# A bias table stored as one row per head, projection tiles among the gating unit's steps, dilated keys multiplied during the first attention, and pooled rows stored ahead of the table's loads

## The reference

```python
def mixer(x):                     # x (1024, 1024) for the prompt, (8, 1024) for the samples
    qa, ka, va, fa, ub, vb, qc, kc, vc, pd = split(x @ w_in)      # 2052 columns
    logf = log_sigmoid(fa + b_forget)
    o_a = forgetting_attention(qa, ka, va, cumsum(logf))          # 4 heads x 64, causal
    v = layer_norm(gelu(vb), g, b)                                # per token, 256 channels
    o_b = gelu(ub) * (tril(w_spatial) @ v + b_spatial)            # per 128-token chunk, 4 groups
    o_c = dilated_attention(qc, kc, vc, t5_table)                 # offsets (128,1),(512,4),(2048,16)
    o_d = pooled(pd) @ w_pool                                     # trailing means 2/4/8/16 minus pd
    return (sigmoid(x @ w_gate) * branches(o_a, o_b, o_c, o_d)).sum(-2) @ w_out
x = layer_norm(ALPHA * x + mixer(x)); x = layer_norm(ALPHA * x + moe(x))   # 16 experts, top 2
```

## Time and profile before

| | |
|---|---|
| median of 3 runs | 1512.75 us (1506.55 to 1513.86) |
| the profiled execution | 1514.06 us |
| its span, first to last instruction | 1512.1 us |
| PE busy | 1371.3 us (91%) |
| PE waits over 2 us named below | 10.4, 9.4 and 2.7 us |
| chain that ended last | PE 83%, DMA 5%, DVE 4%, ACT 3% |

### The profile page before, as it was taken

One profiled execution on the slowest core, in us unless ns is written; L12 is line 12 of the kernel. 1 busy time (PEld: TensorE's weight loads), 2 busy tenths in 40 slices (PEclk: granted clock), 3 DMA queues, 4 the chain that ended last, 5 costly groups with the idle time before them and its releaser, 6 DMA issues.

```text
span 1512.1 us, 20414 instructions
## 1 busy us (share of the span) xinstructions
PE 1371.3 (91%) x7682; PEld 1094.0 (72%) x7682; DVE 779.9 (52%) x1336; ACT 480.7 (32%) x788; POOL 322.8 (21%) x233
## 2 busy tenths in 40 slices
PE   6989989979788999999999999999928999999970
PEld 5665565756555799999999999778826666677640
DVE  3465474542245422344444344464775677777746
ACT  3311145421136311111111111221125556555636
POOL 0258910353453000000000000000245112223220
PEclk9989999999979999999999999999959999999995
DMA  7347620355601121321321431422387998887645
GB/s 226 117 134 263 212 98 1 107 182 169 221 17 32 64 81 63 108 80 64 107 80 65 144 126 66 150 78 79 122 311 280 379 310 312 297 310 254 202 153 226
DMA packets 75197, 237.72 MB, mean 157 GB/s; under 512 B 17029, under 2 KB 27476, under 8 KB 61422
## 3 DMA queue, kind: packets, MB, share of 16 engines
q1 hardware_dynamic: 48630, 160.73, 29.7%
q0 software_dynamic: 17792, 59.20, 13.2%
q10 hardware_dynamic: 8704, 16.84, 3.2%
HBM read 213.49 MB, written 65.74 MB: 185 GB/s over the span
## 4 chain that ended last, share of the span: by engine, by line
PE 83%; DMA 5%; DVE 4%; ACT 3%; issue 2%; POOL 2%; SPq 0%; DVEq 0%; POOLq 0%
PE ps L481 16%; PE ps L483 16%; PE ps L482 16%; PE ps L620 7%; PE ps L1257 6%; PE ps L1229 5%; PE ps L1253 2%; PE ps L1354 2%; PE ps L1254 2%; PE ps L1397 2%; PE ps L1255 2%; DMA b<-in_state_k 2%; PE ps L545 1%; DMA out_pool_p<-b 1%; DMA tmp_yd<-b,b 1%
## 5 line engine op out<-in xcount | busy, mean ns | idle before, releaser
L481 PE MATMUL ps<-b,b 128*128 128x344 f32 (+1 forms) x1360 | 469.1, 345 | 5.4 <-DVE b L841 2.7
L483 PE MATMUL ps<-b,b 128*128 128x344 f32 (+1 forms) x1360 | 465.1, 342 | 0.0
L482 PE MATMUL ps<-b,b 128*128 128x344 f32 (+1 forms) x1360 | 464.9, 342 | 0.0
L481 PEld LDWEIGHTS ps<-b,b 128*128 128x128 f32 x1360 | 254.9, 187 | 24.5 <-issue 3.5
L483 PEld LDWEIGHTS ps<-b,b 128*128 128x128 f32 x1360 | 254.6, 187 | 19.2 <-issue 0.9
L482 PEld LDWEIGHTS ps<-b,b 128*128 128x128 f32 x1360 | 254.6, 187 | 17.2 <-issue 0.9
L1012 DVE TENSOR_TENSOR b<-b,b 128x2048 fp32r<-128x2048 f32 x64 | 146.6, 2291 | 66.2 <-ACT b L704 60.0
L649 ACT ACTIVATE b<-ps,b 128x344 f32<-128x344 f32 x96 | 52.7, 549 | 380.2 <-PE ps L483 380.2
L1083 POOL DMA_INDIRECT tmp_xs<-b,b x36 | 43.1, 1198 | 593.1 <-issue 572.4
L1229 PE MATMUL ps<-b,b 128*128 128x128 f32 (+1 forms) x782 | 119.1, 285 | 39.2 <-DMA b<-tmp_xs 18.4
L1229 PEld LDWEIGHTS ps<-b,b 128*128 128x128 f32 (+1 forms) x782 | 93.0, 145 | 83.4 <-issue 35.6
(11 more groups left out here) (290 smaller groups left out, 1556.0 us busy)
## 6 DMA issues: line engine op xcount, KB each, us to landing
b<-in_w SPq DMA_DIRECT2D x96, 1024.0 KB
b<-in_w_merge SPq DMA_DIRECT2D x32, 640.5 KB, 4.3
tmp_xs<-b ACTq DMA_DIRECT2D x32, 514.0 KB, 4.3
b<-tmp_xs SPq DMA_DIRECT2D x32, 514.0 KB
b<-in_w_in SPq DMA_DIRECT2D x8, 1024.0 KB, 8.8
b<-in_xT SPq DMA_DIRECT2D x4, 1024.0 KB, 11.9
b<-in_w_out SPq DMA_DIRECT2D x4, 1024.0 KB, 8.2
b<-in_x SPq DMA_DIRECT2D x8, 512.0 KB, 4.0
```

The costliest lines, as they stand in the source:

```text
L481: mm(out, hi, mhi, start=start, stop=False)
L482: mm(out, hi, mlo, start=False, stop=False)
L483: return mm(out, lo, mhi, start=False, stop=stop)
```

## The change

- The bias table is computed once per head on 4 partitions (3 matmuls of all 4 heads' columns, 512, 512 and 128 wide), copied by ACT in 3 pieces to `tb_row`, and stored by one transfer that reads each of the 4 rows 128 times. POOL and DVE no longer wait for that store before their next steps; POOL waits for `tb_src` instead.
- "vfa" tiles 2 to 7 and then 0 and 1 are projected between the table, the spatial matmuls and the transposes of `o_b`. The norm of `v` takes two fused instructions per tile in place of three, the first of them already in the loop over tiles.
- The dilated keys of the samples are loaded, multiplied and summed during the first attention (rounds 6 to 13), in a buffer that the key products have left. POOL's later loop holds value gathers alone. ACT's split of the weights of "vpd" starts while the last "qkc" tile is projected.
- The 15 pooling rows are stored before the four loads of the table, and these wait for the last eviction rather than the last projection.
- At the end of the merge the sample tile's split moves to DVE, and all but its last eighth is done before the last merge step.

```diff
-PROJECTED = ([("uv", t) for t in TILE_ORDER] + [("vfa", NT), ("qka", NT)] + [("vfa", t) for t in TILE_ORDER[1:]]
+VFA_ORDER = (2, 3, 4, 5, 6, 7, 0, 1)
+PROJECTED = ([("uv", t) for t in TILE_ORDER] + [("vfa", NT)] + [("vfa", t) for t in VFA_ORDER[:2]] + [("qka", NT)]
+             + [("vfa", t) for t in VFA_ORDER[2:]]
...
-        kc = at(RING + TOKB, [P, 2, 3, W])
+        kc = at(OT + 3 * (TOKB // 4), [P, 2, 3, W])
-        tb_src = at(OT + 4608, [P, 4, TBW])
+        tb_row = at(PSB, [H, TBW])
+        KEYS_C = (6, 7, 8, 9, 10, 11, 12, 13)
...  (end of the merge, PE and DVE)
-                pe.wait_ge(S("mlo"), s + 1)
+                pe.wait_ge(S("mlo"), s + 2 if s else 1)
...
-            for u in range(2):
-                merge_weight(KD // 2 - 1, 3, u, u == 1)
-                split_out_weights(KD - 2 + u, KD - 1 + u)
+            merge_weight(KD // 2 - 1, 3, 0, False)
+            split_out_weights(KD - 2, KD - 1)
+            split_out_weights(KD - 1, KD)
+            first_tile(slice(0, KD - 1))
+            merge_weight(KD // 2 - 1, 3, 1, True)
...  (SP)
-            sp.wait_ge(S("tb_src"), 12)
-            sp.dma_start(a["tb_dram"].rearrange("h (p u) -> p h u", p=P), tb_src[:]).then_inc(S("tb_out"), 16)
+            sp.wait_ge(S("tb_src"), 1)
+            sp.dma_start(a["tb_dram"].rearrange("h (p u) -> h p u", p=P),
+                         tb_row[:].rearrange("h (o u) -> h o u", o=1).to_broadcast([H, P, TBW])).then_inc(S("tb_out"), 16)
...
-            sp.wait_ge(S("proj"), 45)
+            sp.wait_ge(S("evicted"), pj_index("vpd", NT - 1) + 1)
+            sp.dma_start(a["pool_p"], vp[P - 15:P, NT - 1, W:2 * W]).then_inc(S("out_pool"), 16)
             for h in range(H):
                 src = a["tb_dram"][h, P - 1:P - 1 + P * (TBW - 1)].rearrange("(p u) -> p u", u=TBW - 1)[:, 0:SEQ]
                 sp.dma_start(tb[:, h, :], src).then_inc(S("tb_in"), 16)
-            sp.wait_ge(S("evicted"), pj_index("vpd", NT - 1) + 1)
             sp.dma_start(a["v_c_p"].rearrange("(t p) w -> p t w", p=P), vp[:, :, 0:W]).then_inc(S("out_vc"), 16)
-            sp.dma_start(a["pool_p"], vp[P - 15:P, NT - 1, W:2 * W]).then_inc(S("out_pool"), 16)
...  (PE)
-            for h in range(H):
-                for q in range(3):
-                    n = h * 3 + q
-                    if n >= 2:
-                        pe.wait_ge(S("tb_src"), n - 1)
-                    mm(ps[:, 6 + n % 2, 0:384], t5[:, h:h + 1].to_broadcast([NBUCK + 1, P]), oh_rev[:, q * 384:(q + 1) * 384],
-                       start=True, stop=True).then_inc(S("tb_mm"), 1)
+            for n, (lo, hi) in enumerate(TB_PARTS):
+                m = mm(ps[0:H, 5 + n, 0:hi - lo], t5[:], oh_rev[:, lo:hi], start=True, stop=True)
+            m.then_inc(S("tb_mm"), 1)
...
+            project("vfa", NT)
+            project("vfa", VFA_ORDER[0])
+            project("vfa", VFA_ORDER[1])
+            project("qka", NT)
+            spatial(0)
+            spatial(1)
+            project("vfa", VFA_ORDER[2])
+            spatial(2)
+            spatial(3)
+            project("vfa", VFA_ORDER[3])
+            ob_transposes(0, 1)
+            project("vfa", VFA_ORDER[4])
+            ob_transposes(2, 3)
...
+            ob_transposes(6, 7, 8)
+            project("vfa", VFA_ORDER[7])
...  (ACT)
-                    if i == 1:
+                    if t == VFA_ORDER[6]:
                         act.wait_ge(S("obT"), NT + 1)
                         act.wait_ge(S("out_vb"), 16)
...
                 if chunk == "qkc":
-                    act.wait_ge(S("ks"), 16)
-                if chunk == "vpd":
-                    act.wait_ge(S("proj"), pj_index("qkc", NT - 1) + 1)
+                    act.wait_ge(S("ks"), 24)
                 for k in range(KD):
+                    if chunk == "vpd" and k < KD - 1:
+                        act.wait_ge(S("pk"), k + 1)
...  (DVE)
+                v = uv[0:r, t, W:2 * W]
+                dve.scalar_tensor_tensor(v, v, mv[0:r, t, 0:1], gbB[0:r, 0, :], ALU.subtract, ALU.mult)
...
-            for t in range(NT + 1):
+            for t in range(NT, -1, -1):
                 r = rows(t)
                 v = uv[0:r, t, W:2 * W]
-                link(dve.tensor_scalar(v, v, mv[0:r, t, 0:1], rs[0:r, t:t + 1], ALU.subtract, ALU.mult))
-                link(dve.tensor_tensor(v, v, gbB[0:r, 0, :], ALU.mult))
-                link(dve.tensor_tensor(v, v, gbB[0:r, 1, :], ALU.add))
+                m = dve.scalar_tensor_tensor(v, v, rs[0:r, t:t + 1], gbB[0:r, 1, :], ALU.mult, ALU.add)
...
-            dve.wait_ge(S("tb_out"), 16)
             to_oT(1, "ob_tr", "obT")
...
-            last_a = attention(0, lambda h, qt: fb[:, h, 0:P * (qt + 1)], side_a)
+            def side_keys(u):
+                side_a(u)
+                if u in KEYS_C:
+                    key_sums_c(KEYS_C.index(u))
+            last_a = attention(0, lambda h, qt: fb[:, h, 0:P * (qt + 1)], side_keys)
...  (POOL)
-            pool.wait_ge(S("tb_out"), 16)
+            pool.wait_ge(S("tb_src"), 2)
...
-            pool.wait_ge(S("pv"), 8)
+            pool.wait_ge(S("ks"), 16)
             keys_c(0)
             keys_c(1)
             pool.wait_ge(S("sd_qkc"), 16)
             load_q(NB, 0, SC["qkc"])
-            key_step_c(0)
-            key_step_c(1)
+            for b in range(NB):
+                if 0 < b < NB - 1:
+                    pool.wait_ge(S("ks"), 16 + b)
+                    keys_c(b + 1)
+                key_step_c(b)
             for s in range(2, 16):
                 pool.wait_ge(S("dv"), s - 1)
                 load_values(s)
-                if s < NB:
-                    pool.wait_ge(S("ks"), 16 + s - 1)
-                    keys_c(s)
-                    key_step_c(s)
```

More of the change, by code:

```diff
@@ L517, in y_half @@
                 for k in range(KD):
+                    if s == 0 and n == 0 and k == KD - 1:
+                        pe.wait_ge(S("mlo"), 2)
                     if n == 1 and s == 0:
@@ L1255, in project @@
                         m = mm(ps[:, j % 2, :], lo, whi, start=False, stop=(k == KD - 1))
+                        if chunk == "qkc" and t == NT - 1 and k < KD - 1:
+                            m.then_inc(S("pk"), 1)
                     else:
@@ L1275, in _, with spatial @@
+            m.then_inc(S("tb_mm"), 1)
             for i in range(4):
-                m = mm(ps[:, 6, i * H:(i + 1) * H], oh_dec[:, i, :], t5[:], start=True, stop=True)
+                m = mm(ps[:, 4, i * H:(i + 1) * H], oh_dec[:, i, :], t5[:], start=True, stop=True)
             m.then_inc(S("tb_mm"), 1)
-            project("vfa", NT)
-            project("qka", NT)
-            pe.wait_ge(S("wsp_m"), 4)
-            pe.wait_ge(S("v_done"), 1)
-            for g in range(4):
-                if g >= 2:
-                    pe.wait_ge(S("ob"), g - 1)
-                elif g == 0:
-                    pe.wait_ge(S("tb_src"), 13)
+            def spatial(g):
+                if g == 0:
+                    pe.wait_ge(S("wsp_m"), 4)
+                    pe.wait_ge(S("v_done"), 1)
+                    pe.wait_ge(S("tb_src"), 1)
+                elif g >= 2:
+                    pe.wait_ge(S("ob"), g)
@@ L1288, in _, with ob_transposes @@
                 mm(ps[:, 6 + g % 2, :].rearrange("p (t c) -> p t c", t=NT), wsp[:, g, :],
                    uv[:, 0:NT, W + 64 * g:W + 64 * g + 64], start=True, stop=True).then_inc(S("band_mm"), 1)
-            pe.wait_ge(S("ob"), 5)
-            for t in range(NT + 1):
-                if t >= 2:
-                    pe.wait_ge(S("obT"), t - 1)
-                r = rows(t)
-                for f in range(2):
-                    m = tr(ps[:, 4 + t % 2, f * P:f * P + r], uv[0:r, t, f * P:(f + 1) * P], r)
-                m.then_inc(S("ob_tr"), 1)
+            def ob_transposes(*tiles):
+                for t in tiles:
+                    if t == 0:
+                        pe.wait_ge(S("ob"), 5)
+                        pe.wait_ge(S("tb_src"), 2)
+                    if t >= 2:
+                        pe.wait_ge(S("obT"), t - 1)
+                    r = rows(t)
+                    for f in range(2):
+                        m = tr(ps[:, 4 + t % 2, f * P:f * P + r], uv[0:r, t, f * P:(f + 1) * P], r)
+                    m.then_inc(S("ob_tr"), 1)
@@ new lines, in _ @@
+            project("vfa", NT)
[11 more added lines that the diff above has]
+            ob_transposes(2, 3)
+            project("vfa", VFA_ORDER[5])
+            ob_transposes(4, 5)
@@ L1299, in qk_transposes @@
+            project("vfa", VFA_ORDER[6])
+            ob_transposes(6, 7, 8)
+            project("vfa", VFA_ORDER[7])
             def qk_transposes(chunk, t, base):
@@ L1312, in qk_transposes @@
                 m.then_inc(S(f"qk_tr_{chunk}"), 1)
-            for t in TILE_ORDER[1:]:
-                project("vfa", t)
             for i, t in enumerate(TILE_ORDER):
@@ L1630, in _ @@
             act.activation(rs[:], rs2[:], ACT.Sqrt).then_inc(S("sd"), 1)
```

(22 more changed lines are left out.)

42 lines of the change are left out of this document (23 added, 19 removed).

## The result

| | before | changed |
|---|---|---|
| median | 1513.3 us (4 runs) | 1556.28 us (4 runs, 1555.53 to 1557.55) |
| ratio | | 1.0289, 95% interval 1.0259 to 1.0319 |
| span of the profiled execution | 1512.1 us | 1554.9 us |

A forecast was written before the change was run, and what follows sets the result against it. PE (busy 91%) was taken as the engine to shorten, with POOL's key products limiting from 90 to 200 us. Terms -2 -11 +3 -14 -2 = -26 took 1514.06 to 1488, forecast 1487 on the median, range 1478 to 1497.

The forecast's parts named there:

- the landing of the store: Bias-table store: one engine per source row, four at 25.5 GB/s each, data taking 23 us, landing at about 97.
- rival 2: Bias-table store: four neighbouring rows together get 25.5 GB/s, landing at about 166; 1554 or 1553 us; chance 0.20.
- Price of that landing: Late table store: POOL's first product at 170 instead of 89.97, first attention begins 64 us late.
- First attention's start without the slow store: Table and gating unit: of 14 us gained on PE, 2.8 arrive; taken as -2 (bounds -4 and +1).
- Dilated keys: Leaving POOL's later loop: PE's value-step waits go, -11 (bounds -12, -8); first attention pays +3 (bounds 0, +8).
- Pooled rows: Stored before the table's loads: PE's 10.4 us idle plus 3.6 of clock, -14 (bounds -10, -18).
- End of the merge: Of 2.7 us lost there, one short pair of DVE instructions stays: -2 (bounds -2.7, 0).
- The sum: Whole kernel: terms total -26, 1514.06 becomes 1488, forecast 1487 on the median, range 1478 to 1497.

The follow-up runs named there:

- 128 rows: Changed kernel with the table's rows computed on 128 partitions, each stored 4 times, instead of 4 partitions 128 times: 1482.44 us, ratio 0.9801.
- the probe: Kernel before with seven 2304 KB stores added behind its end, read from 4 to 128 partitions: 92.2 us from 4 neighbouring, 5.9 from 128.
- the value tiles together: Kernel on 128 rows with the value tiles projected together behind the gating unit, as before the change: 1473.23 us, ratio 0.9748.

## Why the prediction was wrong

- **The step that failed** is the landing of the store: "So I take one engine per row, four in all", each at 25.5 GB/s, landing at about 97. The count of engines was right (24% of 16). Their rate was not: four neighbouring source rows have 25.5 GB/s together, and the store landed at 164. That is rival 2, which stood at 0.20 and gave 1553; 1556.28 was measured. That these are so near is in part luck: 70.5 us were lost where it had 64, and 27.7 won behind that where it had 24. The row that spoke against it, the 8 packets of the earlier trace rows, was a load into SBUF of one packet per partition with no stream behind it. By their recorded times these 8 packets moved 76 GB/s to eight neighbouring partitions, more than the 51 of the store from eight; why a load should do better was not tested, and it was no row to size a store by. The rule that spoke for the rival (the Trainium skill, "SBUF — State Buffer", Door 1) has 27.6 GB/s, measured, for partitions 0 to 3; the trace now has 25.5. Against it I had no row of a store with few source rows, and a fifth was too small a chance.
- **Price of that landing.** Named: POOL's first product at 170 and 64 us late; measured 169.04 and 70.5. POOL's part was right: its fifteenth product ended at 261.9. What had no price was PE's own path, and it came out longer: 61.4 us behind `out_vb` in the same queue, two tiles of "qka", 25.2 behind the forget gates, then six more tiles up to the first score, with about 3 us of waiting in all. The two waits also cost clock: a tile of "qka" takes 7.03 us where the granted clock is 1.00 (100 to 197 in the kernel before), and took 8.86 behind the second wait, at 0.76 (206.7 to 216.5).
- **First attention's start without the slow store.** Forecast: third product 111.3, first score 196.3, 16th sum ended 201.6, a gain of 2.8. Measured on 128 rows: 109.08, 196.93, 202.55, a gain of 2.2. Right in number, and in part in its reason: the 14 us of PE time do meet a chain of POOL and DVE. But they meet it at the fifth key sum, not at the end of the 16 products. PE stops there for 15.6 us and then runs to its first score with about 3 us of waiting in all. I did not see that stop, nor that the interleaving itself costs 9.2.
- **Dilated keys.** -11 for PE's waits, measured -12.6 with the early split of the weights; +3 in the first attention, measured +2.7 to +3.1. Right.
- **Pooled rows.** -14, measured -13.5 alone and -14.3 in the stage with the rest. The wait as foretold, the clock only in part: foretold was near 1.0 for 25 us where the earlier trace rows has 0.73, and measured were 0.93 with this edit alone, 0.86 on 128 rows (399 to 424) and 0.80 in the changed kernel (473 to 498).
- **End of the merge.** -2, measured -3.3 by the profiles, 0.6 past its bound of -2.7.
- **The sum** without the slow store, 1487, was measured at 1482.44, inside its own range of 1478 to 1497 (28.9 below the kernel before on the same chip, where 26 was forecast). The upper end of that range does not follow from the bounds: +1, -8, +8, -10 and 0 add up to -9, which is 1504 and not 1497. The 1482.44 are inside either way.

## What to carry to other kernels

A store is sized by its bytes and by the SBUF partitions it reads: in all seven stores of the probe no four neighbouring partitions gave more than some 25.5 GB/s together, however often their rows were repeated, and spreading the rows (here for no instruction more than one small copy) gives the rate back. A slow transfer must be priced by what stands behind it in its queue and by what else uses its engines. And engine time saved ahead of a chain that another engine sets is to be followed until it arrives; where it does not, look at the written order of the engine between them.

## What the runs showed of the hardware beyond that

- A transfer from four neighbouring partitions slows other queues too: in the kernel with the store on ACT's queue, 16 KB took 18 us to land, and a gather of keys 21.3 instead of 5.9.
- Some of DVE's small operations take far longer while POOL multiplies. The copy within SBUF below does, and so does the forget gates' first step above (3.64 us at 200.30, beside POOL's product at 199.37). Key sums do not: in the changed kernel one took 2.29 us beside a product (173.58) and one 2.28 without (272.91). Nor did a copy out of PSUM, 0.41 us for 128x256 at 216.81, beside a product. Why was not tested. With the value tiles together, a copy of 128x480 took 4.96 us beside a product of POOL, and 0.41 without one in the kernel on 128 rows; these rows are of the two kernels in that order:

```profile
89.30 4.96 DVE L1873 COPY b<-b 128x480 f32<-128x480 f32 x1
```

```profile
103.14 0.41 DVE L1887 COPY b<-b 128x480 f32<-128x480 f32 x1
```
